# Layer-norm sums moved to GpSimd, and three pieces of reordering, in a two-block attention kernel on one core

## The reference

```
h = x @ w_in                      # block 1: queries 512, keys/values 256, rope 64, gates, pooling
q  = rms_norm(x_q)  @ w_uq        # sum of squares over 512 features
kv = rms_norm(x_kv) @ w_ukv       # sum of squares over 256 features
... causal attention, 4 heads; pooling branch; silu gates ...
x = layer_norm(alpha * x + mix @ w_out)          # mean and variance over 1024 features

proj = h @ w_in_2                 # block 2: q_a, c_kv, q_idx (4 x 64), k_idx (64), w_idx (4), gate_a,
                                  #          q_h, f_h, i_h, gate_h
s_idx = sum_h relu(q_idx . k_idx / 8) * w_idx / 2     # index score of each key
sel = top 256 keys by s_idx;  attention over them and 16 meta tokens
hgrn2: gated linear recurrence over q_h, f_h, i_h (4 heads)
h = layer_norm(alpha * h + y @ w_out_2)
```

## Time and profile before

| | |
|---|---|
| median of 3 runs | 4267.09 us (4260.99 to 4270.25) |
| profiled execution | 4259.95 us |
| its span | 4258.2 us |
| TensorE busy | 3913.5 us, 92% |
| VectorE busy | 1794.8 us, 42% |
| ScalarE busy | 1476.0 us, 35% |
| GpSimd busy | 265.0 us, 6% |
| mean granted TensorE clock | 0.953 |

### The profile page before, as it was taken

How to read it: one execution, slowest core, us unless ns; L and a number is a source line. 1 busy time by engine, 2 the same in 40 slices (tenths; PEclk the granted TensorE clock), 3 DMA queues, 4 the chain that set the end, 5 groups by cost and what they waited for, 6 DMA issues and landing times.

```text
span 4258.2 us, 41374 instructions
## 1 busy us (share of the span) xinstructions
PE 3913.5 (92%) x15538; PEld 2252.0 (53%) x15538; DVE 1794.8 (42%) x4182; ACT 1476.0 (35%) x2458; POOL 265.0 (6%) x328
## 2 busy tenths in 40 slices
PE   7899999999999999999889898899789998788996
PEld 3345644654565456455554445644457744346772
DVE  3313222312222132136532676417785417776631
ACT  1213311322231223123321554305664405774441
POOL 0001001000100010011100111001010001010000
PEclk8999999999999999999889998999889999898998
DMA  4120023002201200322021110111100111110011
GB/s 152 53 91 19 1 69 104 1 20 79 75 1 45 79 30 1 107 74 72 20 75 55 62 55 1 60 57 64 45 20 1 60 59 55 38 35 1 1 39 41
DMA packets 70919, 204.16 MB, mean 48 GB/s; under 512 B 6296, under 2 KB 7872, under 8 KB 70464
## 3 DMA queue, kind: packets, MB, share of 16 engines
q1 hardware_dynamic: 61344, 183.67, 12.9%
q10 hardware_dynamic: 9376, 17.84, 1.1%
HBM read 184.69 MB, written 16.79 MB: 47 GB/s over the span
## 4 chain that ended last, share of the span: by engine, by line
PE 80%; ACT 8%; DVE 7%; issue 3%; DMA 1%; SPq 0%; POOL 0%; ACTq 0%; DVEq 0%; POOLq 0%
PE bank L1589 35%; PE o_acc L1943 6%; PE o_acc L1716 6%; PE bank L1684 5%; PE bank L1911 4%; PE bank L1688 3%; ACT ql L914 3%; PE bank L1807 2%; PE bank L1709 2%; PE bank L1935 2%; PE bank L1597 2%; PE bank L1636 2%; PE bank L1841 2%; ACT prob_t L1044 2%; PE bank L1915 1%
## 5 line engine op out<-in xcount | busy, mean ns | idle before, releaser
L1589 PE MATMUL bank<-group_even,weights 128*128 128x512 f32 x1376 | 607.1, 600 | 16.0 <-DMA weights<-in_w_in_kv 11.5
L1589 PE MATMUL bank<-group_odd,weights 128*128 128x512 f32 x1376 | 603.0, 596 | 5.9 <-ACT tmp L900 5.9
L1589 PE MATMUL bank<-y_all,weights 128*128 128x512 f32 x1024 | 447.7, 599 | 11.8 <-DMA weights<-in_w_out 5.3
L1589 PEld LDWEIGHTS bank<-group_even,weights 128*128 128x128 f32 x1376 | 263.0, 193 | 340.2 <-issue 340.2
L1589 PEld LDWEIGHTS bank<-group_odd,weights 128*128 128x128 f32 x1376 | 261.2, 192 | 329.0 <-issue 328.8
L1170 DVE CUSTOM_DVE_ANT_0 probs<-bank,mask 128x512 f32<-128x512 f32 x256 | 161.5, 687 | 417.8 <-PE bank L1688 417.8
L1589 PEld LDWEIGHTS bank<-y_all,weights 128*128 128x128 f32 x1024 | 196.3, 192 | 258.6 <-issue 258.6
L1943 PE MATMUL o_acc<-v,prob_t 128*128 128x64 f32 x2176 | 290.3, 282 | 45.5 <-ACT prob_t L1044 45.5
L1943 PEld LDWEIGHTS o_acc<-v,prob_t 128*128 128x128 f32 x2176 | 269.6, 197 | 77.9 <-ACT prob_t L1044 77.9
L1044 ACT ACTIVATE prob_t<-bank 128x512 f32<-128x512 f32 (+3 forms) x320 | 160.2, 531 | 392.0 <-PE bank L1935 392.0
L854 ACT ACTIVATE prob_t<-bank 128x512 f32<-128x512 f32 x256 | 145.9, 596 | 430.2 <-PE bank L1709 430.2
(11 more groups left out here) (343 smaller groups left out, 4881.5 us busy)
## 6 DMA issues: line engine op xcount, KB each, us to landing
weights<-in_w_in SPq DMA_DIRECT2D x101, 512.0 KB, 3.5
weights<-in_w_in_q SPq DMA_DIRECT2D x64, 512.0 KB, 3.5
weights<-in_w_out SPq DMA_DIRECT2D x64, 512.0 KB, 3.5
weights<-in_w_i SPq DMA_DIRECT2D x20, 512.0 KB, 3.6
group_even<-in_x_t SPq DMA_DIRECT2D x8, 1024.0 KB, 7.9
group_odd<-in_x_t SPq DMA_DIRECT2D x8, 1024.0 KB, 9.1
group_even<-x_t SPq DMA_DIRECT2D x8, 1024.0 KB, 8.3
group_odd<-x_t SPq DMA_DIRECT2D x8, 1024.0 KB, 7.2
```

The costliest lines, as they stand in the source:

```text
L1589: ins = M(bank(*name)[:], ring[n % SLOTS][:, k * P:(k + 1) * P], rhs[:, k, :], start=(k == 0), stop=(k == chunks - 1))
```

## The change

Five edits.

1. Sums on GpSimd. For a mean, a variance and `q_sq`, GpSimd first adds the chunks with each other (`sum_features`, `sum_squares`, `sum_query_squares`), and PE multiplies the one sum with `ones`: 1 matmul in place of 8 or 4. `sum_features` starts as soon as `residual` has written chunk 1, and writes its total into `probs`. The very last variance (`2var` of group 3) keeps its 8 matmuls.
2. Index weights in key's tile. The weight columns of `ki` held the 64 key columns twice; the second half now holds the 4 index-weight columns, repeated. DVE copies the tile's upper half to the other half of `ki` and the rest to `o_sb` (3 copies of 64 rows in place of 1 of 128), and `wi` becomes 4 transposes in place of 32 matmuls.
3. `f` 0 stands ahead of `2var`.
4. Key products reordered. `kv` tile 0 of the next group stands between `kv_sq` and `k_nope`; `lat` is split in halves for it.
5. `gate2` 0 moves from pair 1 (ahead of level 4) to pair 0, next to `c`, ahead of level 7. In pair 1 the other three move up, and nothing stands ahead of level 6.

```diff
 def first_pair_steps(g):
-    yield from [("kv", g, j) for j in range(2)]
+    if g == 0:
+        yield ("kv", g, 0)
+    yield ("kv", g, 1)
     yield ("krope", g)
     yield ("kv_sq", g)
+    if g + 1 < G:
+        yield ("kv", g + 1, 0)
     yield from [("k_nope", g, h) for h in range(H1)]
...
-    gate_h = [[("gate_h", g, j)] for j in range(3)] + [[("c", g)]]
+    gate_h = [[("gate_h", g, j)] for j in range(3)] + [[("c", g), ("gate2", g, 0)]]
+    gate2 = [[("gate2", g, 1)], [("gate2", g, 2)], [], [("gate2", g, 3)]]
...
-    yield from [("ki", g), *norm["2mean"], ("qi", g, 0), ("qi", g, 1), *norm["2square"], ("wi", g), *norm["2var"], ("f", g, 0), *first[0],
+    yield from [("ki", g), *norm["2mean"], ("qi", g, 0), ("qi", g, 1), *norm["2square"], ("wi", g), ("f", g, 0), *norm["2var"], *first[0],
...
-    yield from heads_steps(g, 1, [[("qa", g, j)] for j in range(4)] + [[("gate2", g, j)] for j in range(4)], ql)
+    yield from heads_steps(g, 1, [[("qa", g, j)] for j in range(4)] + gate2, ql)
...
+            def sum_features(tag, g):
+                total, x_t = probs[:, 0:TB], x_of(g)
+                wait_drained(pool, tag + "out", g, 0)
+                for c in range(1, KC):
+                    wait_drained(pool, tag + "out", g, c)
+                    ins = pool.tensor_tensor(total, x_t[:, 0, :] if c == 1 else total, x_t[:, c, :], ALU.add)
+                    if c < KC - 1:
+                        sum_of(pool, ins)
+                ins.then_inc(ln_summed, 1)
+            def sum_squares(tag, g, sq):
+                base = KC * (g + (0 if tag == "1" else G))
+                for c in range(1, KC):
+                    pool.wait_ge(squared, base + c + 1)
+                    ins = pool.tensor_tensor(sq[:, 0, :], sq[:, 0, :], sq[:, c, :], ALU.add)
+                    if c < KC - 1:
+                        sum_of(pool, ins)
+                ins.then_inc(ln_summed, 1)
+            def sum_query_squares(g):
+                for j in range(1, 4):
+                    pool.wait_ge(q_sq_made, 4 * g + j + 1)
+                    ins = pool.tensor_tensor(y_of(g)[:, 0, :], y_of(g)[:, 0, :], y_of(g)[:, j, :], ALU.add)
...
                     elif kind == "ki":
                         wait_tile(dve, *st)
-                        drains(V.tensor_copy(ki[:, g * TB:(g + 1) * TB], bank(*st)[:]), *st)
+                        for e in range(2):
+                            step(dve, V.tensor_copy(ki[e * DH2:(e + 1) * DH2, g * TB:(g + 1) * TB], bank(*st)[0:DH2, :]))
+                        drains(V.tensor_copy(o_sb[DH2:P, :], bank(*st)[DH2:P, :]), *st)
...
             def mean_of(tag, g):
-                for c in range(KC):
-                    wait_drained(pe, tag + "out", g, c)
-                squares((tag + "mean", g), x_of(g), KC)
+                pe.wait_ge(ln_summed, ln_sums(tag, g, 0))
+                squares((tag + "mean", g), probs[:, 0:TB].unsqueeze(1), 1)
             def variance_of(tag, g, sq):
+                if (tag, g) != ("2", G - 1):
+                    pe.wait_ge(ln_summed, ln_sums(tag, g, 1))
+                    squares((tag + "var", g), sq, 1)
+                    return
...
-                for j in range(4):
-                    wait_drained(pe, "xq", g, j)
-                squares(("q_sq", g), y_of(g), 4)
+                pe.wait_ge(q_summed, g + 1)
+                squares(("q_sq", g), y_of(g), 1)
...
                     elif kind == "wi":
+                        wait_drained(pe, "ki", g)
                         claim(*st)
                         for b in range(BG):
-                            for k in range(KC):
-                                ins = M(bank(*st)[:, b * HI:(b + 1) * HI], x_of(g)[:, k, b * P:(b + 1) * P], w_wi[:, k, :],
-                                        start=(k == 0), stop=(k == KC - 1))
+                            ins = nc.tensor.transpose(bank(*st)[:, b * DH2:(b + 1) * DH2], o_sb[DH2:P, b * P:(b + 1) * P],
+                                                      ident[DH2:P, DH2:P])
```

More of the change, by code:

```diff
@@ L431, in program @@
         brk = alloc(two, "brk", [P, 5, BG])
-        w_wi = alloc(two, "w_wi", [P, KC, HI])
         mx = alloc(two, "mx", [P, H2, 8])
@@ L703, in _, with ln_sums @@
             sp.wait_ge(stored2, 16 * G)
+        def ln_sums(tag, g, var):
+            return 2 * (g + (0 if tag == "1" else G)) + var + 1
         @block.gpsimd
@@ L713, in _ @@
             for g in range(G):
+                if g > 0:
+                    sum_features("1", g - 1)
+                sum_query_squares(g)
+                if g > 0:
+                    sum_squares("1", g - 1, sq_view(probs))
                 for j in range(4):
@@ L775, in rope_tables, with latents @@
                 A_(sin[:], sin[:], ACT.Sin).then_inc(rope_made, 1)
-            def latents(tag, g, n, sq, gain, before):
-                for j in range(n):
+            def latents(tag, g, features, sq, gain, before, at=0):
+                for j in features:
                     wait_tile(act, tag, g, j)
-                    step(act, A_(sq[:, j, :], bank(tag, g, j)[:], ACT.Square))
+                    ins = A_(sq[:, j, :], bank(tag, g, j)[:], ACT.Square)
+                    if tag == "xq":
+                        ins.then_inc(q_sq_made, 1)
+                        act.wait_ge(q_sq_made, 4 * g + j + 1)
+                    else:
+                        step(act, ins)
                     if j == 0 and before is not None:
                         wait_tile(act, *before)
-                    drains(A_(lat[:, j, :], bank(tag, g, j)[:], ACT.Copy, scale=vec[:, gain + j:gain + j + 1]), tag, g, j)
+                    drains(A_(lat[:, at + j, :], bank(tag, g, j)[:], ACT.Copy, scale=vec[:, gain + j:gain + j + 1]), tag, g, j)
             def root(name, width, e, free=None):
@@ L794, in _, with kv_latents @@
                 rope_tables(g)
-                if g > 0:
-                    wait_tile(act, "kv_sq", g - 1)
-                latents("kv", g, 2, prob_t, VEC["kv_g"], ("v", g - 1, BG - 1) if g else None)
+                def kv_latents(a, features):
+                    latents("kv", a, features, prob_t, VEC["kv_g"], ("v", a - 2, BG - 1) if a > 1 else None, 2 * (a % 2))
+                kv_latents(g, range(0 if g == 0 else 1, 2))
                 root(("kv_sq", g), KVR, 0, (k_normed, g) if g else None)
+                if g + 1 < G:
+                    kv_latents(g + 1, range(1))
                 for b in range(BG):
@@ L823, in _ @@
                 rope_tables(G + g)
-                latents("xq", g, 4, y_of(g), VEC["q_g"], ("v", G - 1, BG - 1) if g == 0 else ("mix", g - 1, 3))
+                latents("xq", g, range(4), y_of(g), VEC["q_g"], ("v", G - 1, BG - 1) if g == 0 else ("mix", g - 1, 3))
                 if g > 0:
@@ L1114, in _ @@
                 step(dve, V.reciprocal(rstd[:], std[:]))
[L1115 removed]
+                kv_lat = lat[:, 2 * (g % 2):2 * (g % 2) + 2, :]
+                V.tensor_tensor(kv_lat, kv_lat, wide(rstd[:], 2), ALU.mult).then_inc(k_normed, 1)
                 for h in range(H1):
@@ L1601, in _ @@
             for g in range(G):
-                wait_x(pe, g, g // 2)
-                for j in range(2):
-                    project(("kv", g, j), x_of(g), KC)
+                if g == 0:
+                    wait_x(pe, g, 0)
+                    project(("kv", g, 0), x_of(g), KC)
+                project(("kv", g, 1), x_of(g), KC)
                 project(("krope", g), x_of(g), KC)
@@ L1615, in _ @@
                     for j in range(2):
-                        ins = M(bank(*name)[:], w_ukv[:, j, h * P:(h + 1) * P], lat[:, j, :], start=(j == 0), stop=(j == 1))
+                        ins = M(bank(*name)[:], w_ukv[:, j, h * P:(h + 1) * P], lat[:, 2 * (g % 2) + j, :], start=(j == 0), stop=(j == 1))
                     ins.then_inc(tile_ready, 1)
@@ L2013, in lay_out @@
     w2 = np.asarray(inp["w_in_2"])[0]
-    cols2 = [c0 + ar(P), ki0 + np.tile(ar(DH2), 2)] + [qi0 + j * P + ar(P) for j in range(2)]
+    cols2 = [c0 + ar(P), np.concatenate([ki0 + ar(DH2), wi0 + np.tile(ar(HI), DH2 // HI)])] + [qi0 + j * P + ar(P) for j in range(2)]
     for start in (q0, ga0, hq0, hf0, gh0):
```

27 lines of the change are left out of this document (21 added, 6 removed).

## The result

The changed kernel takes 4155.05 us (median of 4 runs, 4150.67 to 4163.66) against 4264.04 us for the kernel before in the same session (4258.73 to 4270.25): a ratio of 0.9746, 95% interval 0.9723 to 0.9769. That is 109 us less. The prediction had 160 less and a range that ended at 4150, so its direction was right and its size was not.

A forecast was written before the change was run, and what follows sets the result against it. TensorE (PE) was taken as the bound, busy 3913.5 of 4258.2 us. The terms 46.4 + 63.3 + 12 + 8 + 5 + 23.2 + 2 = 159.9 us gave a median of about 4107 us, range 4075 to 4150.

The forecast's parts named there:

- block 1's sums: Block 1's mean, variance and `q_sq`: fewer matmuls with `ones` on PE, additions on GpSimd covered; 46.4 us gained.
- the key products: A `kv` tile fills the waits for `lat` ahead of `k_nope` in groups 0 to 2; 23.2 us gained.
- the meta tiles: Mean, centring, squares and variance there form one chain that gets shorter, with PE idling some 5 us; 8 us gained.
- group 0's weights: Block 2, group 0: `wi` by transposes gives 9.0 us and the four tiles behind it 3; 12 us gained.
- The three later starts: Block 2, `ki` to first index row in groups 1 to 3: 23.5 us less, minus 2.4, each; 63.3 us gained.
- ACT's delay of the index drains: Block 2: the variance's root and table loads put the drains 2.4 us behind PE's index row, counted whole three times.
- the moved gate tile: `gate2` 0 moved to pair 0: waits filled there, level 6 uncovered; 2 us gained, bounds 29 lost to 15 gained.
- The sign that I had named: The prediction is wrong if block 2's recurrence stretches grow by more than 15 us together.
- the 10.9 that I had named: Group 3, pair 1: the wait ahead of uncovered level 6 would be 10.9 us, so nothing is won there.
- the bisection decides: Rival, chance 0.15: half rounds pulled into pair 0 delay its product, open level 6 stops the clock; 15 to 29 us.
- two half rounds now stand ahead of that product: Pair 0, on DVE and ACT: the product ahead of `kd_t` comes later too; no size given.
- The rule of the Trainium skill: No idle gaps between bursts: uncovered level 6 is a mistake; 3 us in each of three groups, edit about -7.

The follow-up runs named there:

- Run 1: The changed kernel with the second gate's tiles put back one ahead of each of levels 4 to 7 of pair 1: 4110.58 us, ratio 0.9636.
- run 4: The changed kernel with the first `f` tile behind the variance again: 4170.13 us, ratio 0.9781.
- run 3: The changed kernel with the gate tile still moved but the bisection's half rounds kept where the kernel before has them: 4132.62 us, ratio 0.9686.
- run 5: Tiles as in run 1, only the half rounds where the changed kernel has them (14 ahead of the first decayed product): 4128.51 us, ratio 0.9676.
- run 6: The changed kernel with its empty place one level later, gate tiles ahead of levels 4, 5 and 6 of pair 1, none ahead of 7: 4145.81 us, ratio 0.9706.
- run 11: Run 1 again, unchanged, with a profile of its own: 4108.04 us, ratio 0.9623.
- Run 7: Run 1 with 6 and 5 matmuls added in the two longest waits of group 0's attention of block 2: 4124.40 us, ratio 0.9661.
- run 8: Run 1 with the index weights computed as before, from `w_wi` by narrow matmuls: 4154.40 us, ratio 0.9749.
- 14: Run 3 again, unchanged, with a profile of its own: 4120.60 us, ratio 0.9654.

## Why the prediction was right in direction and wrong in size

**The terms that held.** Run 1 has all edits but the gate tile. Ahead of block 2's first level its profile gains 92.4 us (1888.73 to 1796.35); forecast were 46.4 for block 1's sums, 23.2 for the key products, 8 for the meta tiles and 12 for group 0's weights, 89.6 together. By parts of the program it is 26.3 up to the end of the key products, 47.9 from there to the meta tiles' mean, and 18.2 from that mean to the first level (8 and 12 forecast): no large errors cancel. The three later starts gain 66.4 against 63.3. By the medians all of it is 154.2 and, in the repetition, 157.7 against 157.9. Within it, the additions are slower than I took them (1.27 for 1.06 us). PE waits for them at the program's last mean, 2.2 us, and at the meta tiles' variance, where I had allowed 5 us; it is 2.5 in the changed kernel and 5.6 in its repetition:

```profile
1720.19 2.08 PE L1662 MATMUL bank<-y_all,ones 128*128 128x512 f32 x2 [2.54 <-POOL y_all L738]
```

ACT's delay of the index drains, which I had counted whole as 2.4 us a group, stayed nearly hidden: the wait of 5.92 us went to 6.2, not to the 8 to 9 that I had named. The order of the first `f` tile and the variance, to which I gave no price, carries 15.1 us (run 4).

**The step that failed: the moved gate tile.** I put it at 2 us gained, with 29 lost as the worst bound, "because work only changes place". It costs 44.5 by the median of run 1, and the half rounds, which had no price in the sum, make up most of what the recurrence lost. The sign that I had named came true: the recurrence grew by 34.9 us, over the 15 at which I would be wrong. Level 6's new wait in group 0 was 1.3 us as forecast, and 6.2, 7.7 and 7.5 in the others; in group 3 that is less than the 10.9 that I had named, so this wait alone is not where the sum went wrong. The rival that named the half rounds ("the bisection decides") had the right place, and a price of 15 to 29 us. Three things in my working were wrong.

First, "two half rounds now stand ahead of that product" was named and not priced. Runs 3 and 5 price it: pair 0 of groups 1 to 3 is 4.4 to 4.6, 4.9 and 6.1 us longer with the half rounds moved, tile or no tile. A half round more costs 2.2 to 3 us there, and the 15.5 us of run 5 are the greater part of its 25.7. When the half rounds stay (run 3), the tile costs pair 0 nothing in groups 2 and 3, and 3.4 us in group 1: in groups 2 and 3 the bisection, not PE, sets the pace of pair 0.

Second, I let pair 1 win back what pair 0 loses, since it has fewer half rounds. It does not: with the half rounds alone moved (run 5) the recurrence behind pair 0's product is 9.6 us longer in groups 1 to 3. A level's keys are made on DVE in the step before it. So the half rounds that delay level 6 are those ahead of level 5's step, and there are 15 from pair 1's first level to there in the changed kernel and in run 3 alike. The three that left stood behind level 5, where they delayed nothing but the last product: its waits are 5.2 us shorter, and that is all that comes back. PE in the changed kernel at levels 5 and 6, and at the product, group 3:

```profile
3701.01 3.78 PE L1912 MATMUL bank<-ql 128*128 128x128 f32 x16 [4.41 <-DVE ql L1475]
3712.32 3.78 PE L1912 MATMUL bank<-probs 128*128 128x128 f32 x16 [7.53 <-DVE probs L1475]
3715.89 7.61 PE L1654 MATMUL bank<-group_odd,weights 128*128 128x512 f32 x16
3723.33 1.95 PE L1912 MATMUL bank<-probs 128*128 128x128 f32 x16
3731.19 1.97 PE L1927 MATMUL bank<-ident,y_all 128*128 128x128 f32 x8 [5.91 <-DVE y_all L1523]
```

Level 6 follows level 5 after 11.3 us with no half round and no tile between them: it waits for those ahead. The empty place would have been better one level later; run 6, which moves it there with its three half rounds, gets 16 us of the recurrence back.

Third, I had not asked which half round stands ahead of which tile in ACT's queue. Run 1, pair 1 of group 3, levels 0 to 2:

```profile
3599.60 3.48 PE L1912 MATMUL bank<-probs 128*128 128x128 f32 x16 [3.14 <-DVE probs L1475]
...
3602.87 7.29 PE L1654 MATMUL bank<-group_odd,weights 128*128 128x512 f32 x16
3605.13 1.25 ACT L976 ACTIVATE ql<-index,mids 128x1152 bf16<-128x1152 f32 x1 [5.70 <-DVE mids L1415]
3610.20 0.60 ACT L1052 ACTIVATE qa<-bank 128x512 f32<-128x512 f32 x1 [2.48 <-PE bank L1654]
...
3613.37 0.17 DVE L1409 SCALAR_TENSOR_TENSOR counts<-signs,counts 128x4 f32<-128x4 f32 x1 [4.48 <-ACT ql L976]
...
3619.01 2.05 PE L1912 MATMUL bank<-probs 128*128 128x128 f32 x16 [0.20 <-DVE probs L1475]
```

The changed kernel at the same place:

```profile
3639.95 3.78 PE L1912 MATMUL bank<-probs 128*128 128x128 f32 x16 [5.68 <-DVE probs L1475]
...
3643.52 7.95 PE L1654 MATMUL bank<-group_odd,weights 128*128 128x512 f32 x16
...
3651.51 0.60 ACT L1052 ACTIVATE qa<-bank 128x512 f32<-128x512 f32 x1 [11.73 <-PE bank L1654]
3652.00 1.25 ACT L976 ACTIVATE ql<-group_even,mids 128x1152 bf16<-128x1152 f32 x1
...
3654.68 0.17 DVE L1409 SCALAR_TENSOR_TENSOR counts<-signs,counts 128x4 f32<-128x4 f32 x1 [8.21 <-ACT ql L976]
...
3660.25 1.04 ACT L993 ACTIVATE y_all<-y_all 128x1024 f32<-128x1024 f32 x1
3661.32 0.69 DVE L1474 TENSOR_TENSOR probs<-y_all,probs 128x512 f32<-128x512 f32 x1 [2.29 <-ACT y_all L993]
...
3662.79 3.49 PE L1912 MATMUL bank<-probs 128*128 128x128 f32 x16 [2.67 <-DVE probs L1475]
```

In run 1 a half round's signs run while PE computes the tile `qa`. In the changed kernel `qa`'s drain (L1052) stands first: ACT idles 11.73 us for PE, the signs start behind the drain, DVE idles 8.21 us for them, and level 2 starts 22.84 us after level 0 where run 1 needs 19.4. Run 5, with these half rounds and run 1's tiles, has the same wait of 2.67 us ahead of this level 2. It is a matter of the later groups: in the changed kernel PE waits 0.8 and 2.7 us ahead of levels 2 and 3 in group 2, and not at all in group 1.

The rule of the Trainium skill (TensorE: Matmul & The Clock Gate, "Why this matters for your kernels") spoke against this edit, and had the direction right. The trace agrees that the clock falls at such gaps: level 6 takes 3.78 us above, at the lower level of 1.2 GHz, as level 5 does. The 9 us that I had put on that rule would still have been short, since most of the time went into waits, 30.1 us more of them at the levels than in run 1.

**What stays open.** Of the 44.5 us the recurrence has 33.8. The rest, 10.7, lies outside it. Group 0's attention of block 2 is the place that shows it: its two profiles average 17.5 us more in the changed kernel than those of runs 1 and 11. All seven profiles with the moved tile have the long stretch; runs 7 and 8 have it without the tile. What sorts the profiles is where the clock falls, counted from pair 1's first `kd_t` transposition. In seven of the nine profiles with the tile at its old place it falls after 20.1 to 21.2 us and stays low for 31 to 61 us; in the seven with the moved tile, and in run 8, it falls after 22.0 to 23.2 us and stays low for 68 to 113. (Run 7, with its waits filled, is the ninth.) The first low stretch in run 11 and in the changed kernel (columns as above):

```profile
2007.50:2045.00 37.50, 24.72 (x81) 17.51 (x81) 21.25 (x68) 12.30 (x38) 5.02 (x8) 0.50 0.00 1
```

```profile
2013.80:2082.00 68.20, 53.42 (x180) 39.64 (x181) 33.27 (x130) 18.64 (x61) 9.77 (x15) 0.50 0.00 1
```

So the long stretch goes with a later fall of the clock, by 1 to 3 us, and the moved tile with both. No run moves the fall alone: that it is the cause is not shown, nor what the moved tile has to do with it.

## What to carry to other kernels

When an order is made by weights, a moved step moves everything that is spread by them; price the two apart (in the recurrence here 5.5 and 25.7 us), or hold one fixed. Before a tile that covers a wait is taken away, ask on which earlier step the operand of the instruction behind it was queued: it is the work ahead of that step that must be covered. And where two engines hand work to each other in small pieces, try a piece ahead of every drain that waits for a long tile, so that the engine has something to do meanwhile; the rows of level 2 suggest it, but no run here tests it alone.

## What was unexpected of the hardware

- GpSimd's addition of 128x512 took 1.27 us in these chains, where the row that I took the price from had 1.06, with the same shape and type. That row is of a subtraction with a broadcast operand and both operands in one tile; the pooling additions of 521 to 527 columns, also a chain, took 1.05 to 1.06 in either kernel. VectorE beside it is not the reason: 52 of the 56 additions of features had no VectorE instruction beside them and took 1.26 to 1.27 us; the other four took 1.37 to 1.58. Nor is it that the output is an input too: the first of each seven writes to a third place and takes 1.26 us as well. The reason stays open.
- The granted clock of one and the same stretch of instructions came out at 0.65 and at 0.71 in two executions of one kernel, 0.75 and 0.80 in two of another, and PE's busy time went with it. One kernel's medians in two sessions were 12.0 us apart (runs 3 and 14), with this stretch 12.9 us apart in their profiles. That is why the recurrence's lengths, which repeat within 3.1 us, carry the argument.
